# Attention keys and queries of a two-layer hybrid backbone prepared with tokens on the partitions

## What is computed

```python
def mla_q(cq, q_norm, w_uq, qk_norm_q, rope):
    q = (rms_norm(cq, q_norm) @ w_uq).reshape(b, n, MLA_HEADS, MLA_QK)
    return rope_tail(rms_norm(q, qk_norm_q), rope)
def mla_kv(ckv_in, kv_norm, w_ukv, qk_norm_k, rope):
    ckv, k_rope = jnp.split(ckv_in, [MLA_KV_LORA], axis=-1)
    kv = (rms_norm(ckv, kv_norm) @ w_ukv).reshape(b, n, MLA_HEADS, MLA_NOPE + MLA_V)
    k_nope, v = jnp.split(kv, [MLA_NOPE], axis=-1)
    k = jnp.concatenate([k_nope, jnp.broadcast_to(k_rope[:, :, None, :], ...)], axis=-1)
    return rope_tail(rms_norm(k, qk_norm_k), rope), v
```

## Time and profile before

| | |
|---|---|
| median of three runs | 2859.64 us |
| profiled execution, its span | 2859.57 us, 2857.8 us |
| busy: TensorE, VectorE, ScalarE, GpSimd | 93%, 49%, 35%, 3% |
| mean granted TensorE clock | 0.952 |
| DMA, mean over the span | 108 GB/s |

### The profile page before, as it was taken

One profiled execution on the slowest core, in us unless ns is written; L12 is line 12 of the kernel. 1 busy time (PEld: TensorE's weight loads), 2 busy tenths in 40 slices (PEclk: granted clock), 3 DMA queues, 4 the chain that ended last, 5 costly groups with the idle time before them and its releaser, 6 DMA issues.

```text
span 2857.8 us, 38510 instructions
## 1 busy us (share of the span) xinstructions
PE 2644.8 (93%) x16344; PEld 2095.4 (73%) x16344; DVE 1388.5 (49%) x2092; ACT 994.3 (35%) x1541; POOL 80.3 (3%) x108
## 2 busy tenths in 40 slices
PE   4999998989978899989999989999898977889999
PEld 2777777634758877767777768888663767889899
DVE  4333344336776663363332353333435677656654
ACT  2322223323563332223222132222241564344443
POOL 0000000000002200000000000000000002200000
PEclk6999999988988999999999999999997988999999
DMA  5444442100210023424444432222220120024454
GB/s 228 177 177 171 158 157 103 60 30 1 89 59 2 2 90 132 147 74 165 168 169 161 161 126 89 103 96 98 87 89 30 60 74 16 2 101 167 169 185 163
DMA packets 44665, 309.79 MB, mean 108 GB/s; under 512 B 5072, under 2 KB 6224, under 8 KB 7632
## 3 DMA queue, kind: packets, MB, share of 16 engines
q1 hardware_dynamic: 44208, 306.20, 29.2%
q10 hardware_dynamic: 288, 1.14, 0.1%
HBM read 306.27 MB, written 1.05 MB: 108 GB/s over the span
## 4 chain that ended last, share of the span: by engine, by line
PE 84%; DVE 10%; ACT 3%; issue 2%; DMA 1%; SPq 0%; DVEq 0%; ACTq 0%
PE bank L1235 65%; PE bank L1538 7%; PE bank L1251 2%; PE bank L1228 2%; DVE rt L1677 2%; PE bank L1462 2%; PE bank L1484 1%; PE bank L1286 1%; DVE w_lo L1666 1%; DMA ring<-in_wts 1%; PE bank L1264 1%; ACT L816 1%; PE bank L1421 1%; PE bank L1471 1%; DVE u_lo L1706 1%
## 5 line engine op out<-in xcount | busy, mean ns | idle before, releaser
L1666 DVE TENSOR_TENSOR w_lo<-ring,w_hi 128x1024 fp32r<-128x1024 f32 x420 | 511.1, 1225 | 1034.5 <-ACT w_hi L798 1031.3
L1235 PE MATMUL bank<-u_hi,w_hi 128*128 128x512 f32 (+1 forms) x2208 | 818.2, 371 | 83.9 <-DVE w_lo L1666 46.7
L1235 PE MATMUL bank<-u_hi,w_lo 128*128 128x512 f32 (+1 forms) x2208 | 801.8, 363 | 0.0
L1235 PE MATMUL bank<-u_lo,w_hi 128*128 128x512 f32 (+1 forms) x2208 | 799.6, 362 | 0.0
L798 ACT ACTIVATE w_hi<-ring 128x1024 fp32r<-128x1024 f32 x420 | 441.4, 1058 | 956.6 <-PE bank L1235 656.2
L1235 PEld LDWEIGHTS bank<-u_hi,w_hi 128*128 128x128 f32 x2208 | 423.1, 192 | 182.0 <-issue 85.4
L1235 PEld LDWEIGHTS bank<-u_hi,w_lo 128*128 128x128 f32 x2208 | 423.4, 192 | 64.0 <-issue 3.9
L1235 PEld LDWEIGHTS bank<-u_lo,w_hi 128*128 128x128 f32 x2208 | 422.8, 191 | 64.1
L1538 PE MATMUL bank<-work 64*64 64x64 f32 (+1 forms) x3952 | 234.6, 248 | 37.7 <-DVE work L2018 21.4
L1235 PE MATMUL bank<-hidden_hi,w_hi 128*128 128x512 f32 (+1 forms) x704 | 259.3, 368 | 0.0
L1538 PEld LDWEIGHTS bank<-work 64*64 64x64 f32 (+1 forms) x3952 | 222.0, 161 | 49.8 <-POOL work L772 31.7
(11 more groups left out here) (190 smaller groups left out, 2523.3 us busy)
## 6 DMA issues: line engine op xcount, KB each, us to landing
ring<-in_wts SPq DMA_DIRECT2D x288, 1024.0 KB, 4.8
h<-in_x SPq DMA_DIRECT2D x8, 256.0 KB, 11.1
par<-in_par ACTq DMA_DIRECT2D x2, 556.0 KB, 5.7
out<-h SPq DMA_DIRECT2D x8, 128.0 KB, 4.0
cst<-in_cst SPq DMA_DIRECT2D x1, 911.5 KB, 10.7
mod_par<-in_mod SPq DMA_DIRECT2D x1, 96.0 KB, 10.0
cond<-in_c SPq DMA_DIRECT2D x1, 8.0 KB, 1.7
```

Source lines behind the costliest of these rows:

```text
L1235: last = weights.used(pe.matmul(out, lhs[a], rhs[b], start=start and n == 0, stop=stop and n == 2))
L1666: tt(w_lo[:, b % HALVES, :], half_source(n % RING, part), w_hi[:, b % HALVES, :].bitcast(F32), ALU.subtract).then_inc(panel_left[n % RING] ...
```

## The change

Key and query products are made with tokens on the partitions: the latent's tile of 128 tokens is the stationary operand and the weights move. A key tile then has 8 heads side by side, a query tile 4. A sum over a head's elements is a reduction along the free axis on VectorE, roots and reciprocals are of a few columns, and rotation is done on VectorE by products with cosine and signed sine tables (which carry the norm's weights) and an exchange of column groups. Transposes turn four heads at a time into the layout that attention reads, and ScalarE's copy out of PSUM applies the weights of the plain part. The latent's norm becomes a scale of each token: for keys and values it is applied in ScalarE's copies; for queries only to the squares, and it stays out of the scores together with the head's root, as `q_root`, which the exponential takes as its scale. The latent's weights go into the copy of the latent. The latent's own sums are matmuls with a single column of ones. The rotation matrices, spreads and head sums go, and 479 columns of constants with them, while the parameters of a layer get 128 more columns. The key's tail is turned with the gates (48 rows in place of 16). Bodies of loops are shown less indented, blank lines left out.

```diff
-      ("cos", 256), ("sin", 256), ("rot", 32), ("pick", 63)):
+      ("cos", 2 * ROPE), ("sin", 2 * ROPE)):
...
-    for c in range(4):
-        add((l, "nope", c), "a")
     for t in range(4):
+        add((l, "nope", t), "a")
         add((l, "mv", t), "a")
     for c in range(GMC):
         add((l, "spatial", c), "v")
...
+    for half in range(2):
+        for t in range(nt):
+            add((l, "uq", half, t), "a")
     for c in range(12):
...
+        q_root = low[:, 384:416].rearrange("p (t c) -> p t c", c=MH)
+        kv_root, cq_root, kr_sum = low[:, 416:420], low[:, 420:424], low[:, 424:428]
...
+    def latent(key, dst, weight, slot, ww):
+        wait_product(act, key)
+        act.activation(sq[:, slot, 0:ww], bank_of(key)[:, 0:ww], ACT.Square).then_inc(latent_squared, 1)
+        act.activation(dst, bank_of(key)[:, 0:ww], ACT.Copy, scale=weight).then_inc(drained["a"], 1)
+    def latent_root(n, dst, tiles, size):
+        act.wait_ge(latent_summed, 2 * l + n + 1)
+        act.activation(dst[:, 0:tiles], bank[7][:, 4 * n:4 * n + tiles], ACT.Sqrt, bias=eps[:, :],
+                       scale=1.0 / size).then_inc(latent_rooted, 1)
     for i in range(2):
-        key = (l, "ckv", i)
         splits.past((l, "low"), i)
-        wait_product(act, key)
-        square((l, "ckv"), i, bank_of(key)[:, :])
-        act.activation(ckv[:, i, :], bank_of(key)[:, :], ACT.Copy).then_inc(drained["a"], 1)
+        latent((l, "ckv", i), ckv[:, i, :], par_of("kv_norm", i, i + 1), i, T)
     key = (l, "krope")
     splits.past((l, "low"), 2)
     wait_product(act, key)
...
+    act.activation(kr[0:ROPE + 16, 0, :], bank_of(key)[0:ROPE + 16, :], ACT.Copy).then_inc(drained["a"], 1)
     for i in range(3):
-        key = (l, "cq", i)
         splits.past((l, "low"), 3 + i)
+        if i == 2:
+            act.wait_ge(latent_summed, 2 * l + 1)
+        latent((l, "cq", i), cq[:, i, 0:w], par_of("q_norm", i, i + 1), (2 + i) % 4, w)
+        if i == 0:
+            latent_root(0, kv_root, 4, LKV)
+    latent_root(1, cq_root, nt, LQ)
...
+    def token_tile(key, n, scale, cols, dst):
         wait_product(act, key)
...
+        if n >= 4:
+            act.wait_ge(tok_summed, SQUARED[l] + n - 3)
+        act.activation(sq[:, n % 4, 0:cols], bank_of(key)[:, 0:cols], ACT.Square,
+                       scale=scale).then_inc(tok_squared, 1)
+        return act.activation(dst, bank_of(key)[:, 0:cols] if cols < T else
+                              bank_of(key)[:, :].rearrange("p (h c) -> p h c", h=MH), ACT.Copy,
+                              scale=scale if cols == T else 1.0)
+    def token_root(n, ap):
+        act.wait_ge(tok_summed, SQUARED[l] + n + 1)
+        act.activation(ap, ap, ACT.Sqrt, bias=eps[:, :], scale=1.0 / QK).then_inc(tok_rooted, 1)
+    def keep_heads(n, what, t, halves):
+        for half in halves:
+            act.wait_ge(heads_turned, TURNED[l] + n + 1)
+            dst = (kk if what == "k" else qq)[0:QK, 4 * half:4 * half + 4, t * P:(t + 1) * P]
+            act.activation(dst, heads(bank[4 + n % 2][0:QK, :]), ACT.Copy,
+                           scale=par_of("qk_" + what, rows=slice(0, QK))).then_inc(heads_kept, 1)
+            n += 1
+    act.wait_ge(latent_ready, 2 * l + 1)
+    for t in range(6):
+        if t < 4:
+            key = (l, "nope", t)
+            if t >= 2:
+                act.wait_ge(heads_turned, TURNED[l] + 2 * (t - 1))
+            last = token_tile(key, t, kv_root[:, t:t + 1], T,
+                              k_tok[:, t % 2, :].rearrange("p (h c) -> p h c", h=MH)[:, :, 0:NOPE])
+            last.then_inc(drained["a"], 1)
+            key = (l, "mv", t)
             wait_product(act, key)
-        square((l, "k"), hd, bank_of(key)[rows, :], slice(0, NOPE))
-        last = act.activation(kk[0:NOPE, hd, :], bank_of(key)[rows, :], ACT.Copy)
-        if hd % 2:
+            act.activation(vm[:, t, :], bank_of(key)[:, :], ACT.Copy, scale=kv_root[:, t:t + 1]).then_inc(drained["a"], 1)
+        if 1 <= t < 5:
+            token_root(t - 1, k_sum[:, (t - 1) % 2, :])
+        if t >= 2:
+            keep_heads(2 * (t - 2), "k", t - 2, (0, 1))
+    act.wait_ge(latent_ready, 2 * l + 2)
+    nq = 2 * nt
+    for i in range(nq + 3):
+        if i < nq:
+            half, t = divmod(i, nt)
+            if i >= 4:
+                act.wait_ge(heads_turned, TURNED[l] + 8 + i - 3)
+            last = token_tile((l, "uq", half, t), 4 + i, cq_root[:, t:t + 1], MH // 2 * QK, q_tok[:, i % 4, :])
             last.then_inc(drained["a"], 1)
...
+        if 1 <= i <= nq:
+            half, t = divmod(i - 1, nt)
+            token_root(3 + i, q_root[:, t, 4 * half:4 * half + 4])
+        if i >= 3:
+            half, t = divmod(i - 3, nt)
+            keep_heads(8 + i - 3, "q", t, (half,))
...
+                           scale=q_root[:, t, hd:hd + 1], bias=nb[:, s:s + 1],
...
+    def latent_sums(n, slots, tiles):
+        pe.wait_ge(latent_squared, 5 * l + (2 if n == 0 else 5))
+        for t in range(tiles):
+            for i, slot in enumerate(slots):
+                last = pe.matmul(bank[7][:, 4 * n + t:4 * n + t + 1], sq[:, slot, t * P:(t + 1) * P], ones[:, 0:1],
+                                 start=i == 0, stop=i == len(slots) - 1)
+        last.then_inc(latent_summed, 1)
...
+    std([(l, "cq", 1), (l, "cq", 2)], w, u, None, 0)
...
+    def turn_heads(n, tile, tile_ready):
+        pe.wait_ge(tok_ready, ROOTED[l] + tile_ready)
+        for half in range(tile.shape[1] // (4 * QK)):
+            if n >= 2:
+                pe.wait_ge(heads_kept, TURNED[l] + n - 1)
+            for hd in range(4):
+                at = (4 * half + hd) * QK
+                last = pe.transpose(bank[4 + n % 2][0:QK, hd * P:(hd + 1) * P], tile[:, at:at + QK], ident)
+            last.then_inc(heads_turned, 1)
+            n += 1
...
-                product_made)
+        for n, what in enumerate(("nope", "mv")):
+            key = (l, what, t)
+            if t == n == 0:
+                wait_drained(pe, (l, "ckv", 1))
+            free_bank(key)
+            product(bank_of(key)[:, :], [(ckv[:, k, t * P:(t + 1) * P], ukv[:, k, 512 * n:512 * n + 512])
+                                         for k in range(2)], product_made)
+        if t == 0:
+            latent_sums(1, (2, 3, 0), nt)
+        if t >= 2:
+            turn_heads(2 * (t - 2), k_tok[:, t % 2, :], t - 1)
...
+        if c == 0:
+            turn_heads(4, k_tok[:, 0, :], 3)
+        elif c == 2:
+            turn_heads(6, k_tok[:, 1, :], 4)
...
+            product(bank_of(key)[:, 0:4 * QK], [(cq[:, k, t * P:(t + 1) * P], uq[:, k, :]) for k in range(3)],
+                    product_made)
+        if i >= 2:
+            turn_heads(8 + i - 2, q_tok[:, (i - 2) % 4, :], 4 + i - 1)
+    pe.wait_ge(heads_kept, TURNED[l] + 8 + nq)
...
+        step(tt(place, other, sine, ALU.mult))
+    if dst is src:
+        step.wait()
+    step(tt(dst, src, table(cos), ALU.mult))
     step.wait()
-    return tt(dst, dst, tmp, ALU.add).then_inc(out_sem, 1)
+    return tt(dst, dst, tmp, ALU.add)
...
+    def latent_inverse(n, ap):
+        dve.wait_ge(latent_rooted, 2 * l + n + 1)
+        dve.reciprocal(ap, ap).then_inc(latent_ready, 1)
...
+    step(dve.tensor_copy(kr_raw, turned[:, :, 0:ROPE]))
+    dve.tensor_copy(gab, turned[:, :, ROPE:48]).then_inc(ab_read, 1)
...
+    def squares_of(n, dst, groups, size):
+        dve.wait_ge(tok_squared, SQUARED[l] + n + 1)
+        return dve.reduce_sum(dst, sq[:, n % 4, 0:groups * size].rearrange("p (h c) -> p h c", c=size), AX.X)
+    def k_sums(t):
+        dst = k_sum[:, t % 2, :]
+        step(squares_of(t, dst, MH, NOPE))
+        step.wait()
+        ts(dst, dst, kr_sum[:, t:t + 1], None, ALU.add).then_inc(tok_summed, 1)
+    def k_scaled(t):
+        r = k_sum[:, t % 2, :]
+        tile = k_tok[:, t % 2, :].rearrange("p (h c) -> p h c", h=MH)
+        dve.wait_ge(tok_rooted, ROOTED[l] + t + 1)
+        step(dve.reciprocal(r, r))
+        step.wait()
+        wait_drained(dve, (l, "nope", t))
+        tt(tile[:, :, 0:NOPE], tile[:, :, 0:NOPE], r.unsqueeze(2).to_broadcast([P, MH, NOPE]), ALU.mult)
+        tt(tile[:, :, NOPE:QK], kr_tok[:, t:t + 1, :].to_broadcast([P, MH, ROPE]),
+           r.unsqueeze(2).to_broadcast([P, MH, ROPE]), ALU.mult).then_inc(tok_ready, 1)
+    for t in range(5):
+        if t < 4:
+            if t >= 2:
+                dve.wait_ge(heads_turned, TURNED[l] + 2 * (t - 1))
+            k_sums(t)
+        if t:
+            k_scaled(t - 1)
...
+    nq = 2 * nt
+    for i in range(nq + 1):
+        if i < nq:
+            half, t = divmod(i, nt)
+            squares_of(4 + i, q_root[:, t, 4 * half:4 * half + 4], MH // 2, QK).then_inc(tok_summed, 1)
+            wait_drained(dve, (l, "uq", half, t))
+            tile = q_tok[:, i % 4, :].rearrange("p (h c) -> p h c", c=QK)[:, :, NOPE:QK]
+            if t < 2:
+                tmp = turns[:, i % 2, :].rearrange("p (h c) -> p h c", c=ROPE)
```

(13 more changed lines are left out.)

233 lines of the change are left out of this document (74 added, 159 removed).

## The result

Four runs took 2748.07 to 2752.49 us, median 2749.74; the kernel before took 2860.03 (2858.6 to 2860.44, four runs). The ratio is 0.9618, with a 95% interval of 0.9606 to 0.9629. The forecast was 2741.0, with a range of 2726 to 2768: 110.3 us came off where 118.7 were forecast. The profiled execution took 2748.07 us, its span 2746.3, against 2859.57 and 2857.8: 111.5 less by either.

A forecast was written before the change was run, and what follows sets the result against it. TensorE held 84% of the chain, so time leaves only where it waits or does removable work. Savings of 63.9 us (layer 0), 54.3 (layer 1) and 0.5 (start) make 118.7 off 2859.57: 2741 us, range 2726 to 2768.

The forecast's parts named there:

- Layer 1's rotation and scaling: Layer 1's latents: TensorE's 2.10 us idle ahead of the key rotation and the rotation's 0.59 both go, 2.7 us.
- The small operations: VectorE's many short operations on latents and query tiles lie beside TensorE; on its path, the query ones would return 17 us.
- The tail of the queries: Behind the last query product nothing covers square, sum, rotation, turn, root and keeps: 3.5 us, 3.7 in layer 1.
- The pointer scalars in it are at a price I take as nothing: Attention's pointer scalars cost nothing under TensorE's cover; without it, 48 heads x 0.09 = 4 us.
- First score to first transposes: Before the first exponential, the next panel's rounding is queued behind the last keep: a loss of 1.2 us a layer.
- The start: Before the first product 180 KB less move: 0.8 us saved at most, nothing at least, 0.5 taken.
- layer 0's rotation: Layer 0's latents: the key rotation on TensorE goes, saving 0.55 us.
- serial tile loops: Key and query tile loops don't overlap, up to 2790 us, half of it 2765; chance 13%.
- clock rival: TensorE's clock falls to 1.2 GHz in the new stage: 60 us more, 2801, half of it 2771; chance 7%.
- More gain: The third key tile's wait (2.7 us) and the query tail (2 us) vanish in both layers: 2730 us; chance 8%.
- slower rival: Clock still 1.2 GHz when attention starts and stays there, adding 130 us: 2871; chance 1%.
- DMA rival: The change saves nothing because the wait only shifts to the next panels' DMA; chance 1%.

The follow-up runs named there:

- four key tiles: Key tiles and their sums get four buffers instead of two, and two waits for turning go, against the changed kernel: 2739.59 us, ratio 0.9583.
- the first fill: Three 128x512 products with unread results put behind TensorE's third score, against the changed kernel: 2749.99 us, ratio 0.9618.
- the fixed scale: Exponential and negative maximum take a number, not a pointer, so the output isn't the reference's; against the changed kernel: 2746.09 us, ratio 0.9608.
- the splits in the middle: In layer 0 ScalarE rounds the next panel after its fourth query tile, VectorE after the last, against the changed kernel: 2747.58 us, ratio 0.9613.
- the version that scales the key latent: Key latent's norm again by spread sums, 128x512 root and reciprocal, and VectorE scaling, against the changed kernel: 2745.98 us, ratio 0.9606.

## Why the prediction was right, and where its terms were off

Right were direction, mechanism and most terms. **Stage, layer 0**: 27.9 us to the first query product, forecast 26.9; a query tile 1.94 + 0.44 = 2.38, forecast 2.44; first score 49.6 behind the projections, forecast 48.6. **Stage, layer 1**: 37.6, forecast 36.5. **The wait in the keys** was foreseen at its place, ahead of the third tile's turns and behind the first spatial product, as 2.7 us; TensorE stood 2.53 in layer 0 and 2.97 in layer 1. From the square's start to the last scaling the chain counts 0.69 + 0.58 + 0.58 + 0.20 on ScalarE and 0.21 + 0.69 + 0.35 on VectorE, and it is ScalarE, late with that square, that TensorE waits for, as the prediction says. **Layer 1's rotation and scaling**: 2.76 for 2.7. **The small operations** of VectorE lie beside TensorE: 49 of them in the query stretch, busy 14.82 of 22.80 us under TensorE's 21.12; one of 128 elements took 286 ns (L1917), as priced. One reading is wrong without effect: x16 in the earlier trace rows is not 8 products and 8 weight loads but 16 matmul records, two to a 128x512 product; the price of 0.88 us a product stands.

The sum has no term for TensorE's clock behind a short wait, and most of what it missed lies there. The terms that were off:

- **The keys behind their wait.** The first query product came 1.0 us late in both layers though the wait was as forecast. The forecast had 4.7 us from the third tile's turns to the first query product in layer 0; it took 6.1 (573.40 to 579.48). The turns of the third tile took 1.94 us and those of the fourth 0.87, and the granted clock is 0.50 from 573.40 to 575.40. In layer 1 the fourth tile's took 1.71. With the shorter wait of four key tiles they take 1.08 and 0.87.
- **The tail of the queries**, from the last query product to the first score: 4.1 and 4.0, forecast 3.5 and 3.7. The query tiles at 2.38 gave 0.5 and 0.2 back.
- **Attention after its first transposes** was taken as unchanged. It is 2.2 us longer in layer 0 and 2.3 in layer 1. In layer 0 the heads over 512 keys take 34.8 us (607.13 to 641.92) for 33.6 before (and 33.1 with the first fill), since the first transposes and scores run at half clock; before, the half clock fell on the first scores, 5.50 us, and from 669 us on the granted clock was 0.99. In layer 1, which has only such heads, the granted clock is 0.50 from 2103.40 to 2109.00, where the kernel before had 1.00 from 2217.00 on; these 5.6 us at half speed are enough for its 2.3.
- **"The pointer scalars in it are at a price I take as nothing".** This failed on its cover, and makes the other 1.0 us of layer 0. TensorE leads the heads over 512 keys, but in the heads over 256 keys the chain reads as below, and a pair of heads takes 3.0 us, 1.5 a head, for 1.43 before. With the fixed scale it is 1.43 again.
- **First score to first transposes** went the other way: 1.2 was to be lost in each layer, and 0.5 was. The first exponential came 4.24 us behind the score, forecast 4.5, and the transposes follow it by 1.64 us for 2.07. The second part was foreseen nowhere; it hides 0.4 of the misses above in each layer, which is luck.
- **The start (0.5) and layer 0's rotation (0.55)** gave nothing in this execution, but the execution hides them. TensorE reached the first half step's products 1.3 us sooner than before (58.49 for 59.76). These 48 then took 13.93 us; in the profile with the fixed scale, the same code up to there, they took 12.87 from the same start. There the third query projection ended at 549.96, 1.5 us sooner than before, and in all eleven profiles of the variants it ended by 551.22. Against that, the stretch from 328.50 us to the rounding at 454.67 took 126.17 us in the changed kernel and in the fixed scale's profile, for 125.63 before; where these 0.5 come from is open.

The chain of the changed kernel in the 256-key heads:

```profile
648.63 0.44 DVE small L2003
...
650.32 0.65 PE bank L1522 x4
...
651.64 0.44 DVE small L2003
```

Added up for layer 0: 1.2 (start and rotation) + 1.0 (first score) + 2.2 (attention) − 0.7 (score to transposes) = 3.7 less than forecast; for layer 1: 1.1 + 2.3 − 0.7 = 2.7. Between the layers 0.9 of the lead was lost and 0.1 came back at the end, which makes 7.2, the difference of 118.7 and 111.5.

**The rivals.** The serial tile loops didn't come: query tiles 2.38 apart. But their mechanism is real, and one position nearer in TensorE's order brings 9.5 us of it; two key buffers brought part of it into the changed kernel. The clock rival came in small. Over the stage it is 0.97 (551.60 to 600.50), far from what the rival needed, but it fell to 0.50 for 2 us behind the wait in the keys and again behind the wait for the splits. "More gain" named the third tile's wait and the tail: four key tiles shorten that wait from 2.5 to 0.5 us, leave the tail as it is, and gave 2739.6. The slower rival decides nothing, since attention's clock is 0.97 and 0.93, and neither does the DMA rival: in these timelines no idle time of TensorE is put down to a panel.

## What to carry to other kernels

Where many small matmuls only gather or spread a row, put the reduced index on the free axis: the stage here fell from 113 to 50 us and from 89 to 38, and the normed factor can go into the scale of an operation that must run anyway. Then look at the circle of buffers first: two more key tiles gave 10 us, the largest gain of all edits tried on the changed kernel, while moving a rounding, filling the clock or saving a pointer gave nothing that could be told in the median. Price what comes behind the new, shorter wait: work that hid under it (here the splits) becomes visible, and the matmuls behind a wait may run at half clock: here they did behind waits of 2.5 to 3 us and not behind those of 0.5 and 0.9 at the same place. And when one profile shows a gain of 1 to 2 us at the place of an edit, follow it to the end of the program: here such gains were gone some stages later.

## What the runs showed of the hardware that was not expected

- A pointer for the scale costs the exponential 91 ns at either size (0.687 to 0.778 and 0.474 to 0.565 us), and a 128x1 product on VectorE 60 ns (154 to 214), with or without a second factor. The Trainium skill, "ScalarE: Activation LUTs", section "What ACT_TABLE_LOAD costs", puts each pointer operand of an ACTIVATE at about 93 ns: the trace agrees.
- Spreads with 8 rows took 1.74 us each (two records of 0.87) with TensorE busy 91% (24.85 of 27.20), at a granted clock of 0.56; query products with 128 rows, 1.94 us a tile, ran at 1.00.
- Idle time and clock: behind 2.53 us of idle TensorE ran 2.0 us at a granted clock of 0.50; behind 0.50 and 0.94 us of idle at the same place it ran at 1.00. No rule comes out of this alone: the first scores of layer 0, behind waits of the same length (1.51 and 0.77 us), ran at full clock in the changed kernel's profile and at half clock in that of the first fill.
- In layer 0, after the latent sums, the same 16 records of key products took 6.97 us in the changed kernel's profile and in that of the splits in the middle, and 8.67 in the others, as in the chain of the version that scales the key latent; in layer 1 they took 6.97 in all:

```profile
555.88 8.67 PE bank L1280 x16
```

Which of the two it is moves a stage by 1.7 us without an edit that bears on it, and it is largely paid back. The two profiles with 6.97 are those whose projections ended last, at 551.63 and 551.22; the six others with two key tiles ended them at 549.9 to 550.8, and the first query product stood at 579.0 to 580.6 in all eight. In the fixed scale's profile the key stage is 1.9 us longer than in the changed kernel's and ends 0.2 us later. The first scores, too, take 2.84 us in some profiles and 5.5 in others. Stages compared from one profile each are no better than this.
